# The end of the second mixer: out-projection products that ask for chunks one head pair older, and a third slab begun behind the last value products

## The reference, cut to what matters

```
x = x + g1 * mix
o_lat = ...                                   # per head: softmax over 64 selected keys, times the latents
o = jnp.einsum('bshl,hlv->bshv', o_lat, w_uv) # 16 heads of 64 = 1024 features
return o.reshape(B, S, 1024) @ w_out          # the out-projection, 1024 x 1024
```

## Time and profile before

| what | value |
|---|---|
| median of 3 runs | 1215.47 us (1215.38 to 1215.55) |
| the profiled execution: its own time | 1215.8 us |
| the profiled execution: span from first to last instruction | 1214.1 us |
| mean granted TensorE clock over the span | 0.982 |
| TensorE busy (matmuls) | 1163.4 us, 96% |
| VectorE busy | 543.6 us, 45% |
| ScalarE busy | 250.1 us, 21% |
| mean DMA rate over the span | 193 GB/s |

### The profile page before, as it was taken

One profiled execution on the slowest core, in us unless ns is written; L12 is line 12 of the kernel. 1 busy time (PEld: TensorE's weight loads), 2 busy tenths in 40 slices (PEclk: granted clock), 3 DMA queues, 4 the chain that ended last, 5 costly groups with the idle time before them and its releaser, 6 DMA issues.

```text
span 1214.1 us, 13985 instructions
## 1 busy us (share of the span) xinstructions
PE 1163.4 (96%) x5765; PEld 1001.1 (82%) x5765; DVE 543.6 (45%) x1056; ACT 250.1 (21%) x458; POOL 23.5 (2%) x82
## 2 busy tenths in 40 slices
PE   3899999999999999998999999999999999999997
PEld 2688888888888878877888888888788888888885
DVE  6255554555564546332455546464733231111113
ACT  2122323000000244542300000025423320000002
POOL 1000140000000000000000000000000000000000
PEclk8899999999999999989999999999999999999998
DMA  9977827787868452270678787754341345353510
GB/s 347 297 260 252 300 74 275 260 312 254 308 236 302 138 70 91 83 243 1 237 254 313 251 310 262 268 184 139 110 133 36 104 131 182 110 202 105 195 47 35
DMA packets 154161, 234.04 MB, mean 193 GB/s; under 512 B 8761, under 2 KB 126577, under 8 KB 154097
## 3 DMA queue, kind: packets, MB, share of 16 engines
q1 hardware_dynamic: 154097, 233.13, 57.0%
HBM read 231.67 MB, written 1.44 MB: 192 GB/s over the span
## 4 chain that ended last, share of the span: by engine, by line
PE 94%; DVE 3%; SPq 1%; ACT 1%; issue 1%; DMA 1%; ACTq 0%; DVEq 0%
PE PS L591 49%; PE PS L658 18%; PE PS L612 7%; PE PS L602 5%; PE PS L752 2%; PE PS L577 2%; PE PS L993 1%; PE PS L563 1%; DVE ada_acc L1476 1%; DMA ffn_work<-in_final_norm_g 1%; PE PS L1067 1%; PE PS L785 1%; PE PS L922 1%; PE PS L768 1%; PE PS L804 0%
## 5 line engine op out<-in xcount | busy, mean ns | idle before, releaser
L591 PE MATMUL PS<-hT,slot 128*128 128x256 f32 x2736 | 606.2, 380 | 4.4 <-ACT hT L1176 3.1
L591 PEld LDWEIGHTS PS<-hT,slot 128*128 128x128 f32 x2736 | 520.1, 191 | 77.4 <-issue 6.8
L658 PE MATMUL PS<-act,slot 128*128 128x256 f32 x1056 | 239.2, 380 | 1.5 <-DVE act L1591 1.5
L658 PEld LDWEIGHTS PS<-act,slot 128*128 128x128 f32 x1056 | 200.1, 190 | 30.9 <-DVE act L1591 2.3
L1562 DVE TENSOR_SCALAR ffn_work<-PS,pcol 128x256 f32<-128x256 f32 x100 | 50.7, 540 | 314.3 <-PE PS L591 314.2
L1476 DVE SCALAR_TENSOR_TENSOR ada_acc<-ada_slot,cond,ada_acc 128x1024 f32<-128x1024 f32 x126 | 161.5, 1282 | 6.2 <-DMA ada_slot<-in_ada_w 0.6
L1228 ACT ACTIVATE ffn_work<-ffn_work 128x256 f32<-128x256 f32 x66 | 27.6, 418 | 615.1 <-DVE ffn_work L1572 615.1
L612 PE MATMUL PS<-oT,slot 128*128 128x256 f32 x384 | 89.5, 395 | 6.2 <-DVE oT L1788 6.2
L612 PEld LDWEIGHTS PS<-oT,slot 128*128 128x128 f32 x384 | 75.6, 199 | 18.4 <-DVE oT L1788 6.9
L602 PE MATMUL PS<-xg,slot 128*128 128x257 f32 (+1 forms) x256 | 57.4, 381 | 2.4 <-DVE xT L1526 2.4
L602 PEld LDWEIGHTS PS<-xg,slot 128*128 128x128 f32 (+1 forms) x256 | 47.6, 187 | 11.3 <-issue 4.0
(11 more groups left out here) (250 smaller groups left out, 744.3 us busy)
## 6 DMA issues: line engine op xcount, KB each, us to landing
ada_slot<-in_ada_w SPq DMA_DIRECT2D x144, 512.0 KB, 7.9
slot<-in_ffn_w_up SPq DMA_DIRECT2D x44, 1024.0 KB, 11.5
slot<-in_ffn_w_down SPq DMA_DIRECT2D x22, 1024.0 KB, 4.9
slot<-in_w_up SPq DMA_DIRECT2D x22, 1024.0 KB, 5.1
slot<-in_sb_w_in SPq DMA_DIRECT2D x12, 1024.0 KB, 7.3
slot<-in_w_in SPq DMA_DIRECT2D x11, 1024.0 KB, 5.1
slot<-in_w_down SPq DMA_DIRECT2D x11, 1024.0 KB, 4.9
slot<-in_dsa_w_in SPq DMA_DIRECT2D x10, 1024.0 KB, 5.3
```

The costliest lines, as they stand in the source:

```text
L591: last = mm(PS[:, bank, half * T:half * T + T], slot[s][:, k, m * P:(m + 1) * P], x[:, k, :], start=k == 0, stop=k == KC - 1)
L658: last = mm(PS[:, c // 2, (c % 2) * T:(c % 2) * T + T], w[:, j_odd * D + c * P:j_odd * D + (c + 1) * P], act[:, j_odd, :], start=start and ...
```

## The change

Only TensorE's stream is edited; no instruction is added or taken away on any other engine, no transfer is moved, and TensorE issues the same 64 products of the out-projection, in another order and behind other waits. Pair 6 asks for the last filling but one of unit 1 to have been read (chunk 4) and does 5 chunks of slab 0 (10 products). Pair 7 asks for chunk 5, does chunk 5 of slab 0 (2 products) and 6 chunks of slab 1 (12). Behind the loop, before the wait for chunk 7, TensorE now asks for chunk 6, does it for the slabs 0 and 1 (4 products), and begins slab 2 with 7 chunks (14 products, slot 5, unit 3). Then it waits for chunk 7 and does the 22 products that are left: 2, 2, 2 and 16.

```diff
--- before.py
+++ after.py
@@ -959,18 +959,23 @@
                 if p < 6:
                     project_q(p + 2)
                 elif p == 6:
-                    was_read(1)
-                    out_start(1, 0, 6)
+                    was_read(1, 1)
+                    out_start(1, 0, 5)
                 else:
-                    was_read(1)
-                    out_start(1, 1, 7)
+                    was_read(1, 1)
+                    out_products(1, 0, (5,))
+                    out_start(1, 1, 6)
                 turn(p, frees=1 if p == 5 else None)
                 if p < 7:
                     scores(p + 1)
                 mix(p)
 
+            was_read(1, 1)
+            out_products(1, 0, (6,))
+            out_products(1, 1, (6,))
+            out_start(1, 2, 7)
             was_read(1)
-            out_projection(1, started=(6, 7))
+            out_projection(1, started=(7, 7, 7))
             ffn(1)
 
             arrived(3)
```

## The result

The changed kernel takes 1206.19 us (median of 6 runs, the lowest 1204.57), against 1214.45 us for the kernel before in 6 runs. The ratio is 0.9931, with a 95% interval of 0.9914 to 0.9949; one of the six, at 1378 us, was a disturbed execution: it is left out of the ratio but not of the median, and the other five have a median of 1204.82. Two later comparisons of the same pair, each on one chip, gave 0.9945 (0.9927 to 0.9963; medians 1206.04 and 1213.55) and 0.9926 (0.9910 to 0.9941; medians 1204.91 and 1214.93).

What follows compares the result with a forecast made beforehand. TensorE was taken as the bound (94% of the chain); old waits and slow groups of 11.6 us less 2.2 of new waits and restarts gave 9.4 off 1215.47, so 1206.0 us, range 1204.0 to 1209.4.

Steps and rivals of the forecast that it cites:

- The total: Whole kernel: median of 1215.47 us less the gain of 9.4 gives 1206.0 us, at chance 0.80.
- The sum of 9.4 us: TensorE around the out-projection: old waits and slow groups, 11.6 us, less new waits and restarts, 2.2.
- Pair 6: Its 10 products start without the 2.84 us wait; a new 1.35 us wait for probabilities follows; gains 5.33 us.
- Pair 7: Wait for oT goes, 0.41 us wait for unit 2 appears; value products end at 556.19, 9.49 us earlier than before.
- Behind the loop: Before the wait for chunk 7, 36 instructions cover VectorE's 0.42 us; all 80 run unbroken in 17.27 us.
- The clock: TensorE's granted clock stays full behind the new short waits of 1.35, 0.41 and 0.99 us; the sum depends on it.
- rival (a): Clock falls behind the new waits too: 1211.2 us if twice, 1207.6 to 1209.2 if once; chance 0.12.
- 5.2 us of clock: Half-speed loss in the old groups behind the two 2.84 us waits: 3.21 + 1.95 us.
- Rival (b): Gain given back behind the out-projection, where three slabs' work falls on VectorE and ScalarE together: 1210.6 us; chance 0.04.
- Rival (c): Another condition, slot or unit, was nearly as late as oT, so no early start: 1215.5 us; chance 0.02.
- Rival (d): Clock stays at half behind the new waits for the rest of the out-projection: slower, up to 1229 us; chance 0.02.

Runs made afterwards that it cites:

- experiment 3: Changed kernel without the third slab's early start: 1209.47 us, ratio 0.9952 to the kernel before; timed again, 1206.24 us, ratio 0.9934.
- experiment 6: Changed kernel with chunk 6's 4 products moved ahead of the last value products: 1205.96 us, ratio 0.9936; also without third slab's early start: 1206.26 us, 0.9932.

## Why the prediction was right, and where it was off

**The total.** 1206.0 was forecast and 1206.2 measured, 1206.0 and 1204.9 in the later comparisons. The sum of 9.4 us was 9.13 in the stretch of the profiled pair. That the total came out to 0.2 is luck: the base of 1215.47 was the median of three runs, and with three more it is 1214.45, 1.0 lower; the medians moved by 8.3 and not 9.4, 1.1 less; and the two nearly cancel. Without the run at 1378 us it would have been 1204.82 that was measured.

**Pair 6**: 5.33 forecast. Its value products end 9.88 us into the stretch and before did so 15.22 us into it: 5.34. The new wait for the probabilities was 1.15 us and not 1.35, because the 20 products end 0.2 later than the steady pace gives (536.49 + 4.58 = 541.07, which is 4.51 us into the stretch and not 4.32). It costs nothing: the probabilities set the start of the transposes, 5.67 us into the stretch, as forecast.

**Pair 7**: from there to the end of its value products 13.35 us before and 9.29 after, 4.06, forecast 4.16. The wait for unit 2 was 0.29 and not 0.41, but again only because the products ahead of it ended later. VectorE gave the unit back when forecast, at 547.17 + 0.48 = 547.65; the products went on 0.14 us behind that, where I had 0.06, and this is the 0.1. The probabilities were early, as forecast: no wait stands before the transposes of pair 7.

**Behind the loop**: the last 80 instructions ran in one row, in 17.46 us where I had 17.27, because they take 0.218 us each here and the 24 of the first mixer, from which I took the pace, 0.216. That is 0.2 of the 0.3 us by which the sum was too large, and pair 7's is the other 0.1.

**The forecast had no reason for the third slab, and there is none in this order.** My step said that 36 instructions cover the 0.42 us of chunk 7; the 8 of chunk 6 do so too (experiment 3). It starts to matter, by 0.6 us, only where chunk 6 is used earlier (experiment 6).

**The clock.** The step that it stays at full behind the three short waits held in all three profiles of the change, and in every other one in which the stretch had no wait above 1.35 us (eight profiles of five kernels). In these, rival (a) did not occur.

By the Trainium skill ("TensorE: Matmul & The Clock Gate", section "A second HAM failure mode: psum-queue depth-cycling") the slow groups could have stayed. The eight profiles show no such swing in the stretch (granted 1.00).

Executions without a profile leave rival (a) open in part. Of the changed kernel's 17 times in its three comparisons (the run at 1378 us aside), those at 1208.42, 1209.71 and 1210.06 us have a mean granted clock of 0.983, where the profiled ones have 0.988 and 0.992. Against 0.988 that is about 12 us more at half speed (0.005 x 2 x 1208, an estimate), and one fall behind the 2.71 us wait is 3.2 us of it. So the clock was at half elsewhere too, or for longer; whether in the stretch, no trace shows.

**What was mis-sized is the base.** I took 5.2 us of clock from one execution and the whole 9.4 off the median of others. The wait of 2.84 us occurred eight times in five profiles (twice in each profile of the kernel before and in that of the third slab alone, once in each with a pair put back), and half speed followed in six, worth between 1.6 and 3.0 us each. Without any fall the stretch of before would be 4.4 us longer than the new one: 45.76 - (8.39 - 5.45) - (8.00 - 6.21) - 36.63. That is worked out and was not seen: all three profiles with both waits have at least one fall, and no trace shows an execution of the kernel before without any. The smallest difference that traces show is 6.2 us (42.8 - 36.6); what comes on top, up to 9.1, depends on the falls. The medians differ by 8.3 (9.6 without the run at 1378 us), 7.5 and 10.0 us. So 9.4 was the price of an execution with both falls, and that the medians moved by nearly as much is in part chance: they also hold the falls of the clock behind the 2.71 us wait, which either kernel may have.

**Rival (b)**, work given back behind the slabs: ScalarE was idle for 4.44 us before the last slab, and the 283.76 us behind the stretch are the same. **Rival (c)**: the early start is there, at 536.49. **Rival (d)**: no profile of the changed kernel has a half-speed piece in the stretch.

## What to carry to other kernels

Where a consumer waits for the newest of a row of results, let it take the older ones first: the wait is then covered by work that was ready, and what counts is the next condition in line (here the probabilities), which bounds the gain before anything is written. A wait on TensorE that is long enough (here 2.71 us and more, in a part of the executions; 1.96 us and less in no profile) costs a second time in the clock behind it; one useful or even useless group of matmuls in it saves that, so read the granted clock behind each wait, not only the waits. And do not price the clock from one profile: take a second of the kernel before, and look at the mean granted clock of the executions that have no profile.

## What the runs showed of the hardware that was not expected

Whether the clock falls behind a wait is not settled by the wait's length alone, and what settles it no run here shows. The same wait, 2.84 us to the hundredth at the same place of the same kernel, was followed by full clock in one execution (24 instructions in 5.45 us, granted 1.00) and by half in another (8.39 us, granted 0.51), and by something between in a third kernel (7.02 us). The wait of 2.71 us in the third layer did the same: in 5 of the 13 profiles half speed followed, and the small matmuls behind it took about 1.6 us longer, as 4.07 to 2.48 us above. Behind the kernel's last wait, of 2.90 us, it followed in all 13. Between the start-up and that wait, waits of up to 1.96 us never had it in these profiles.

This explains much of the scatter of the kernel before, 1210.24 to 1216.33 us. Of those 24 executions the two fastest (1210.24 and 1210.49) have a mean granted clock of 0.991, as the second profile has at 1210.59, and nine between 1215.34 and 1216.33 have 0.982, as the first profile has at 1215.8. Whether it explains all of the scatter stays open, since only one execution of each run was profiled.
